# Two scatter parts ahead of the last down product, and the second half's copy in two pieces

## The reference

```python
for e in range(N_EXPERTS):                      # 32 experts, two chosen per token
    y = (jax.nn.silu(tok @ expert_gate[e]) * (tok @ expert_up[e])) @ expert_down[e]
    out = out + combine[:, e:e + 1] * y.astype(jnp.float32)
```

## Time and profile before

| what | us |
|---|---|
| median of 3 runs | 802.28 |
| lowest, highest | 802.28, 802.77 |
| the profiled execution | 803.42 |
| its span in the trace | 801.6 |
| PE busy | 772.7 (96%) |
| DVE busy | 309.8 (39%) |
| ACT busy | 205.9 (26%) |
| HBM read | 252.86 MB, 317 GB/s over the span |

### The profile page before, as it was taken

The page is one execution under the profiler, slowest core; times in us unless marked ns, Lnnn a source line. Parts: engine busy times, 40 slices in busy tenths (PEclk is TensorE's granted clock), DMA queues, the critical chain, the costliest instruction groups (busy, mean ns, idle before and its releaser), DMA issues.

```text
span 801.6 us, 16500 instructions
## 1 busy us (share of the span) xinstructions
PE 772.7 (96%) x6464; PEld 546.5 (68%) x6464; DVE 309.8 (39%) x738; ACT 205.9 (26%) x440; POOL 3.2 (0%) x12
## 2 busy tenths in 40 slices
PE   9999999999999999799999999999999999999966
PEld 8887788878755555366588778888787555555423
DVE  4776343663611211111167754346635111111112
ACT  2352541532400000000124544326212000100003
POOL 0000000000000000000000000000000000000000
PEclk9999999999999999899999999999999999999998
DMA  9983264498699999999998532656888999999996
GB/s 343 417 267 97 89 235 158 150 382 341 228 423 417 421 420 419 421 421 420 418 415 301 180 105 67 224 197 226 350 321 315 421 421 420 420 420 422 419 422 246
DMA packets 44905, 256.57 MB, mean 320 GB/s; under 512 B 5088, under 2 KB 12576, under 8 KB 16032
## 3 DMA queue, kind: packets, MB, share of 16 engines
q1 hardware_dynamic: 44256, 254.77, 80.5%
q10 hardware_dynamic: 576, 0.81, 0.3%
HBM read 252.86 MB, written 1.64 MB: 317 GB/s over the span
## 4 chain that ended last, share of the span: by engine, by line
PE 71%; DMA 13%; DVE 8%; ACT 5%; issue 2%; DVEq 0%; ACTq 0%; SPq 0%; POOL 0%; POOLq 0%
PE ps L654 13%; PE ps L1117 13%; PE ps L1080 7%; DMA late_buf<-e_down 7%; PE ps L980 7%; PE ps L1142 6%; DMA ring<-e_down 4%; DVE xn L1508 3%; PE ps L1150 3%; PE ps L1154 3%; DMA shapes<-e_gate 3%; PE ps L871 2%; PE ps L840 2%; PE ps L682 2%; PE ps L826 1%
## 5 line engine op out<-in xcount | busy, mean ns | idle before, releaser
L654 PE MATMUL ps<-hT,ring 128*128 128x256 f32 x800 | 183.6, 382 | 1.1 <-DVE hT L1540 0.9
L654 PEld LDWEIGHTS ps<-hT,ring 128*128 128x128 f32 x800 | 148.5, 190 | 24.8 <-issue 4.7
L1080 PEld LDWEIGHTS ps<-picked,xn 128*128 128x128 f32 x624 | 74.8, 193 | 17.8 <-issue 15.2
L1080 PE MATMUL ps<-picked,xn 128*128 128x128 f32 x624 | 83.4, 283 | 2.4 <-ACT xn L1419 1.4
L1117 PE MATMUL ps<-space,hT 128*32 128x256 f32 x992 | 64.2, 397 | 11.3 <-DMA space<-e_up 7.2
L1882 DVE TENSOR_TENSOR hT<-ps,gffn 128x512 f32<-128x512 f32 x38 | 26.3, 692 | 113.0 <-PE ps L1080 113.0
L1445 ACT ACTIVATE hT<-ps 128x256 f32<-128x256 f32 x18 | 6.9, 383 | 223.0 <-PE ps L1117 223.0
L980 PE MATMUL ps<-xn,ring 128*128 128x256 f32 x256 | 58.2, 382 | 0.0
L1117 PEld LDWEIGHTS ps<-space,hT 128*32 128x32 f32 x992 | 29.9, 113 | 38.5 <-DMA space<-e_up 11.0
L1142 PE MATMUL ps<-ring,space 128*32 128x512 f32 x416 | 51.5, 599 | 1.9 <-DMA ring<-e_down 1.9
L980 PEld LDWEIGHTS ps<-xn,ring 128*128 128x128 f32 x256 | 48.0, 190 | 7.1 <-issue 0.7
(11 more groups left out here) (288 smaller groups left out, 883.3 us busy)
## 6 DMA issues: line engine op xcount, KB each, us to landing
ring<-e_down SPq DMA_DIRECT2D x46, 1024.0 KB, 26.6
ring<-w_mix SPq DMA_DIRECT2D x33, 1024.0 KB, 8.9
ring<-e_up SPq DMA_DIRECT2D x28, 1024.0 KB, 11.5
space<-e_gate SPq DMA_DIRECT2D x26, 1024.0 KB, 21.4
space<-e_up SPq DMA_DIRECT2D x24, 1024.0 KB, 23.8
ring<-e_gate SPq DMA_DIRECT2D x18, 1024.0 KB, 26.4
more_buf<-e_gate SPq DMA_DIRECT2D x8, 1024.0 KB, 8.2
late_buf<-e_down SPq DMA_DIRECT2D x8, 1024.0 KB, 26.0
```

The costliest lines, as they stand in the source:

```text
L654: mm = pe.matmul(bank, slot_w(i)[:, k, ct * P:(ct + 1) * P], hT3[:, k, :], start=(k == 0), stop=(k == KD - 1))
L1080: mm = pe.matmul(ps[:, 4 + k // 4 * 3, k % 4 * P:(k % 4 + 1) * P], xn3[:, j, k * P:(k + 1) * P], Psel[:, j, :], start=(j == 0), stop=(j == ...
```

## The change

Three things are edited. `scatter(0, 1)` moves from behind `down(1, 1)` to ahead of it. DVE copies half 1 in two pieces of 256 columns, each with its own increment of `y1_ready`. And PE takes half 1's scatter in two steps, each with a wait for its piece: in layer 0 these are `scatter(1, 0)` and `scatter(1, 1)` as before, in layer 1 each step has one product with 256 columns for j = 1 and one for j = 0, in place of one product with 512 columns for each j.

```diff
+                        def second_half():
+
+                            for c in range(2):
+                                pe.wait_ge(y1_ready, 2 * n + c + 1)
+                                if l + 1 < LAYERS:
+                                    scatter(1, c)
+                                else:
+                                    cs = slice(256 * c, 256 * c + 256)
+                                    for j in (1, 0):
+                                        mm = pe.matmul(ps[:, 2 * j + 1, cs], PwT[:, j * P:(j + 1) * P], ysb[:, 1, cs],
+                                                       start=False, stop=False, skip_group_check=True)
+                                        if c:
+                                            mm.then_inc(sums, 1)
+
                         down(0, 0)
                         down(0, 1)
                         down(1, 0)
                         pe.wait_ge(y0_ready, n + 1)
                         scatter(0, 0)
+                        scatter(0, 1)
                         down(1, 1)
-                        scatter(0, 1)
-                        pe.wait_ge(y1_ready, n + 1)
-                        scatter(1, 0)
-                        scatter(1, 1)
+                        second_half()
                         pe.reg_add(rounds, rounds, 1)
...
                         dve.wait_ge(slot_done, n * QSLOTS + 12)
-                        dve.tensor_copy(ysb[:, 1, :], ps[:, 6, :]).then_inc(y1_ready, 1)
+                        for c in range(2):
+                            dve.tensor_copy(ysb[:, 1, 256 * c:256 * c + 256], ps[:, 6, 256 * c:256 * c + 256]).then_inc(y1_ready, 1)
                         dve.reg_add(rounds, rounds, 1)
```

## The result

| | us |
|---|---|
| changed kernel, median of 12 runs | 805.51 |
| kernel before, median of the runs beside it | 802.47 |
| ratio, 95% interval | 1.0032, 1.0025 to 1.0039 |
| profiled execution of the changed kernel, its span | 806.09, 804.3 |

The changed kernel is slower by 0.32% (0.25% to 0.39%), which is +2.6 us (2.0 to 3.1). This document goes by the ratio on record; the two medians in the table lie 3.0 us apart. The forecast was +1.3 us and "within 0.2%" as the likeliest case.

What follows compares the result with a forecast made beforehand. DMA transfers were taken to bound the expert stages, so only what follows each layer's last transfers counts: 0.66 (layer 0's tail) + 0.63 (layer 1's) = +1.3 us, 802.28 to 803.6 us; range 801.9 to 805.3.

Steps and rivals of the forecast that it cites:

- likeliest case: Whole kernel: +1.3 us, 0.16% slower, within the 0.2% that cannot be told from no change; chance 0.52.
- slower by over 0.2%: Whole kernel: clock drop at the end (+3.0 us, 0.15) or a dearer gap (1.4 us more, 0.21); together 0.36.
- What bounds the kernel: Expert stages: full DMA engines set the length, later buffers do not empty the queue, so the two layer tails count.
- A round's end: Round without waits, both layers: 5.45 us against 4.87, +0.58 per round, with 0.42 for the copy's first piece.
- Layer 0's tail: Last round of layer 0: PE's room used up over two rounds, `down(1, 1)` 0.94 late, less 0.28: +0.66 us.
- Layer 1's tail: End of layer 1: `down(1, 1)` +0.46, ACT's squares of j = 1 at 795.68 instead of 795.05, +0.63 us.
- The second piece is covered: DVE's second copy piece ends at most 0.42 us on, beside the first piece's scatter of 1.06, in both layers.
- PE is what the next layer's chain hangs on: Behind layer 0's tail: DVE's copies end somewhat later, but the next layer's chain follows PE; no added cost.
- the mixer only shifts: Layer 1: loads wait for its mixer's buffers, so its expert stage shifts with layer 0's tail; no added cost.
- The rival of the clock: Last down products of layer 1: half clock on 790.5 to 795 adds 1.7 us, +3.0 in all, 805.3 us; chance 0.15.
- the moved gap moves the drop: End of layer 1: by the skill's rule on bursts between DMA waits, a moved gap moves PE's drop to half clock.
- The Trainium skill's rule against short copies: DVE's copy in pieces: fixed latency per instruction, 0.16 us per tail, 0.3 in both; taken as covered by the scatter.

Runs made afterwards that it cites:

- last_quads: Against the kernel before: the whole change in the last quad of each layer alone, old order and whole copy elsewhere; 1.0017, +1.4 us.
- first_quads: Against the kernel before: the whole change in all but the last quad of each layer, which keeps the old order and whole copy; 1.0006, +0.5 us.
- move_only: Against the kernel before: only `scatter(0, 1)` moves ahead of `down(1, 1)`, one whole copy and the old second half; 1.0026, +2.1 us.
- pad_before: The kernel before with one more register instruction (an addition of 0) per quad's loop on DVE; 804.36 us in one execution, beside 802.39.
- second comparison: The changed kernel itself run once more against the kernel before; 1.0024 (1.0014 to 1.0034), +1.9 us.
- change_look2: The changed kernel unaltered, one more profiled execution; 803.86 us, the kernel before beside it 802.39.

## Why the prediction was partly wrong

**The direction and the mechanism held, the size did not.** The range for the time, 801.9 to 805.3, holds the 804.8 that the ratio makes of the 802.28 of before. Against the runs beside it, the median of 805.51 lies just above. The likeliest case, within 0.2%, did not come; slower by over 0.2% had 0.36. That the time still fell into the range owes something to luck: the range was that wide for rivals which did not come true as described.

1. *What bounds the kernel.* Right: DMA share 1.01 in the stages, 15 us of queue bear buffers that come free later (SP's longest wait for them went from 9.7 to 12.4 us, without effect), and the loss sits at the two tails. `last_quads` (+1.4) against `first_quads` (+0.5) shows it, with intervals that overlap.
2. *A round's end.* 5.46 measured, 5.45 forecast; the copy's piece 420 ns against 0.42. Column for column, 256 cost what 512 did (1.92 to 1.93 for half 1).
3. *Layer 0's tail.* +0.70 in the first profile, +0.72 to +0.74 in four from a landing on, against 0.66, with the interplay that PE's room of two rounds is used up by the gap. `last_quads` (+0.16 against 0.13) and `move_only` (+1.8 against 1.7) confirm the parts. `first_quads` confirms them only once its clock is accounted for.
4. *Layer 1's tail.* +0.63 as forecast, 3.21 in the first profile and 3.21 or 3.22 in the three others.
5. *The second piece is covered.* Right for PE: its scatter starts at the first piece's end.
6. *"PE is what the next layer's chain hangs on" was the step that failed.* It held from 403 to 415. Behind that DVE is on the chain, and there the idle piece of 0.25 became 0.62: +0.34. I had costed the copy's edit at what the copy does where it stands, and had said that the mixer only shifts. The sum that the profiles support is 0.70 + 0.34 + 0.63 = 1.7. The cause of the 0.34 is open.
7. *The rival of the clock.* I had given it 0.15, and 1.7 us on the down products themselves. What the runs showed is an earlier and smaller blow: a drop from about 780 or 782 that lasts to 787 or 789 stretches the gather ahead of the down products, 1.1 in one profile of the changed kernel, 0.3 in another, 0 in two. I had not looked at the one in layer 0 from about 326, which cost 0.6 more in the second of them. The drop comes in the old order too (`pad_before`), and so is not brought by the change alone; the change removed the waits that had taken up part of it. The Trainium skill, "TensorE: Matmul & The Clock Gate", section on HAM oscillation, on bursts between waits on DMA, fits what the rows show: the half clock began in a stretch of waits in the profiles shown. That the moved gap moves the drop, as I had drawn from it, is not shown.
8. *The Trainium skill's rule against short copies* ("VectorE: DVE Perf Modes", the TRN2 errata) is borne out in its number, 2 x 0.420 - 0.692 = 0.15 per copy by the mean durations; in the timeline the pair takes 0.76, 0.07 more than the one copy. No tail shows a cost of it.

1.7 us lies within the second comparison (+1.1 to +2.7) and under the first (+2.0 to +3.1). What the first has beyond it, 0.3 at the least, stays open. The long drop accounts for its profiled execution, but not for all of the rest. The mean granted clock is on record for every execution of the changed kernel: it was 0.999 in two of the first comparison's twelve and in four of the second's eight, and `change_look2`, which has the same mean, shows no window of 20 us below 0.99, so a drop of 7 us has no room in them. Those two took 804.85 and 804.99, 2.4 and 2.5 above the 802.47 beside them; those four took 803.74 to 804.93 beside 802.44. The kernel before never had more than 0.995 where its clock is on record.

## What to carry to other kernels

Work that is moved ahead into a wait must be shorter than the wait, measured where it ends last: here 0.86 us of products went into gaps of 0.42 and 0.46. What it had covered behind stands bare then, so weigh both sides: the move alone cost 2.1 us, and half of it, which fits the gap and leaves cover behind, together with the copy in pieces cost nothing that could be told. And a bare wait costs the copy (0.42), the two handovers (0.13 and 0.06), and the weight load that can no longer run ahead (0.2, the 1.06 of a part behind an exposed load against 0.86). A wait that is used up also no longer absorbs what else makes PE late, such as a drop of its clock.

## What the runs showed of the hardware that was not expected

- Idle time on DVE ahead of an instruction far from the edit was 0.62 us, not 0.25, in every kernel with one more copy or more in its code, and stayed at 0.25 with eight more register instructions.
- In the last round the half clock (0.50) lasted 3.4 us from 782 in one execution of the old order and 6.8 us in another; in the changed kernel it was there in two profiles, for nearly 7 us, and absent in two. It cost from nothing to 1.1 us in that round, and 0.6 us in layer 0, by where the next wait stood.
- Executions of one kernel are apart before they reach the edited code: layer 0's first gather started at 211.84 to 212.86 in the four profiles of the changed kernel. Tails must be compared from a landing to the end, within one execution.
